# Both norm borders around a feed forward, worked in two halves of 256 tokens

## The reference, cut to what matters

```python
    h = h + rmsnorm(mixed @ w_out, g_mix_post)            # border 1, unit "wo" ahead of it
    hn = rmsnorm(h, g_ffn_pre)
    f = jnp.square(jax.nn.relu(hn @ w_ff1)) @ w_ff2       # units "f1" and "f2"
    h = h + rmsnorm(f, g_ffn_post)                        # border 2
...
    ada = silu(c) @ ada_w + ada_b                         # worked out beside the feed forward
    h = rmsnorm_2(x, norm1_g) * (1.0 + sc1) + sh1
    z = h @ w_in                                          # units "cin", "lat", "ga", "gc"
```

## Time and profile before

| | us |
|---|---|
| median of 3 runs | 1757.79 (1756.8 to 1762.38) |
| the profiled execution | 1757.74 |
| its span, first to last instruction | 1755.7 |
| mean granted TensorE clock | 0.977 |
| PE busy | 1664.1 (95%) |
| DVE busy | 1189.1 (68%) |
| ACT busy | 735.0 (42%) |
| POOL busy | 340.0 (19%) |

### The profile page before, as it was taken

How to read it: one execution, slowest core, us unless ns; L and a number is a source line. 1 busy time by engine, 2 the same in 40 slices (tenths; PEclk the granted TensorE clock), 3 DMA queues, 4 the chain that set the end, 5 groups by cost and what they waited for, 6 DMA issues and landing times. The chain is left out here.

```text
span 1755.7 us, 19580 instructions
## 1 busy us (share of the span) xinstructions
PE 1664.1 (95%) x8098; PEld 1322.3 (75%) x8098; DVE 1189.1 (68%) x1541; ACT 735.0 (42%) x955; POOL 340.0 (19%) x193
## 2 busy tenths in 40 slices
PE   5999899899999998999999988999999999999997
PEld 4878787777888886888887877878755776777775
DVE  5979768872333438953466446767965657899998
ACT  4253445444312243221222214334376237677774
POOL 1000011214100002500000004434501004445452
PEclk9999999899999998999999997999999999999999
DMA  5535223433322232445335421222210205999995
GB/s 213 194 116 167 71 64 107 149 98 121 108 96 96 96 144 100 167 165 192 143 121 192 161 104 54 73 96 96 96 44 5 73 0 212 383 386 391 385 360 189
DMA packets 59639, 264.49 MB, mean 151 GB/s; under 512 B 21648, under 2 KB 22288, under 8 KB 33056
## 3 DMA queue, kind: packets, MB, share of 16 engines
q1 hardware_dynamic: 34896, 159.10, 25.1%
q0 software_dynamic: 15184, 99.90, 14.5%
q10 hardware_dynamic: 9472, 4.26, 0.9%
HBM read 239.80 MB, written 23.44 MB: 150 GB/s over the span
## 5 line engine op out<-in xcount | busy, mean ns | idle before, releaser
L376 PE MATMUL bank<-h_high,wsplit 128*128 128x512 f32 x992 | 320.6, 401 | 10.8 <-DVE h_low L2070 4.9
L1583 DVE TENSOR_TENSOR wsplit<-ring,wsplit 128x2048 fp32r<-128x2048 f32 x75 | 174.3, 2324 | 161.3 <-ACT wsplit L968 161.2
L968 ACT ACTIVATE wsplit<-ring 128x2048 fp32r<-128x2048 f32 x98 | 187.1, 1909 | 205.2 <-PE bank L376 192.5
L376 PEld LDWEIGHTS bank<-h_high,wsplit 128*128 128x128 f32 x992 | 188.3, 190 | 57.7 <-ACT h_high L1298 5.1
L376 PE MATMUL bank<-xn_high,wsplit 128*128 128x512 f32 (+1 forms) x832 | 217.2, 348 | 12.1 <-DVE xn_low L1614 8.0
L376 PE MATMUL bank<-h_low,wsplit 128*128 128x512 f32 x496 | 197.5, 398 | 0.0
L376 PEld LDWEIGHTS bank<-xn_high,wsplit 128*128 128x128 f32 x832 | 145.6, 190 | 34.7 <-DVE xn_low L1614 8.1
L376 PE MATMUL bank<-f_high,wsplit 128*128 128x512 f32 x512 | 168.2, 401 | 0.0
L376 PE MATMUL bank<-xn_low,wsplit 128*128 128x512 f32 (+1 forms) x416 | 143.8, 346 | 0.0
L1583 POOL TENSOR_TENSOR wsplit<-ring,wsplit 128x2048 fp32r<-128x2048 f32 x23 | 106.6, 4635 | 175.6 <-ACT wsplit L968 175.5
L2617 POOL TENSOR_TENSOR x<-x,z 128x512 f32<-128x512 f32 x8 | 11.6, 1444 | 554.3 <-DVE z L2058 554.3
(11 more groups left out here) (500 smaller groups left out, 3314.9 us busy)
## 6 DMA issues: line engine op xcount, KB each, us to landing
ring<-in_W SPq DMA_DIRECT2D x122, 1024.0 KB, 4.8
weights_out<-prep SPq DMA_DIRECT2D x8, 864.0 KB, 5.2
prep<-weights_out_early POOLq DMA_DIRECT2D x8, 576.0 KB, 3.1
xslot<-zeros SPq DMA_DIRECT2D x7, 516.0 KB, 5.1
block<-xslot SPq DMA_DIRECT2D x6, 516.0 KB, 12.2
yslot<-block_out SPq DMA_DIRECT2D x6, 512.0 KB, 8.8
prep<-turns_early POOLq DMA_DIRECT2D x8, 288.0 KB, 2.4
x_in<-in_xT SPq DMA_DIRECT2D x4, 528.0 KB, 7.7
```

Source lines behind the costliest of these rows:

```text
L376: return g.matmul(o, l, r, start=first, stop=last_, skip_group_check=True)
L968: g.activation(wst[:, side(n), 0, :], ringt[:, n % RING, :], ACT.Copy).then_inc(*a.sig(("high", n)))
L1583: g.tensor_tensor(wst[:, side(n), 1, :], ringt[:, n % RING, :], hi, SUB).then_inc(*t.sig(("low", n), ("released", n)))
```

## The change

The two borders are worked in halves of 256 tokens. Ahead of border 1 the unit wo_3 is computed for z0 and then for z1, and behind it f1_0 and f1_1 go z0, z0, z1, z1 (`in_halves`). Ahead of border 2 it is f2_14 and f2_15 (f2_14 for z0 and z1, then f2_15 for both), and behind it cin_0 and cin_1 in the same pattern. The sums, roots, inverses, spreads, residuals and splits are halved alike. For z1 the sum and the spread stand on PE within the first unit behind the border, after input block 3 and block 6. The low parts of cin_1 and cin_2 move from POOL to DVE, POOL's low parts of h at border 2 move to DVE, and the positions are now loaded when the last low part of z1 is done.

```diff
-POOL_LOW = {UNIT[p] for p in [("zg", i) for i in range(4)] + [("zs", 0), ("zs", 1)] + [("cin", i) for i in (1, 2, 3)]
+POOL_LOW = {UNIT[p] for p in [("zg", i) for i in range(4)] + [("zs", 0), ("zs", 1)] + [("cin", 3)]
...
+            def sum_half(name, z, x, first=True, last=True):
+                b = fresh(name, z) if first else banks.at(name, z)
+                for m in range(2):
+                    t = mm(b[:, m:m + 1], x[:, 128 * m:128 * m + 128], ones[:, 0:1], first and m == 0, last)
+                t.then_inc(*p.sig((name, z)))
+                if last:
+                    banks.close(name, z)
+            def spread_half(name, z):
+                b = fresh(name, "scale", z)
+                p.wait_ge(*at("inverse", name, z))
+                for m in range(2):
+                    t = mm(b[:, 128 * m:128 * m + 128], rt4[:, 2 * z + m:2 * z + m + 1].to_broadcast([128, 128]), ident, True, True)
+                t.then_inc(*p.sig((name, "scale", z)))
+                banks.close(name, "scale", z)
+            def in_halves(name, xh, xl, rows, beside):
+                for z in range(2):
+                    for i in range(2):
+                        n = UNIT[name, i]
+                        wh, wl = weights(n, 8, 2048)
+                        p.wait_ge(*at("low", n))
+                        grown = [fresh(name, 2 * i + j, z)[:, 0:256] for j in range(2)]
+                        for k in range(8):
+                            p.wait_ge(*at(rows, k, z))
+                            for j in range(2):
+                                m = slice(128 * j, 128 * j + 128)
+                                t = three(grown[j], wh[:, k, m], wl[:, k, m], xh[:, k, TK[z]], xl[:, k, TK[z]], k == 0, k == 7)
+                                if k == 7:
+                                    t.then_inc(*p.sig((name, 2 * i + j, z), ("used", n)))
+                            beside(z, i, k)
+                        for j in range(2):
+                            banks.close(name, 2 * i + j, z)
...
+                        if (z, i, j) == (1, 3, 0):
+                            p.wait_ge(*at("mix_post", "square", 7, 0))
+                            sum_half("mix_post", 0, nrm[:, 2, TK[0]])
+            spread_half("mix_post", 0)
             p.end("end", "wo", "pe")
-            sum_by_token("mix_post", nrm[:, 2, :], first=7)
-            spread_scale("mix_post")
...
+            def wo_second(z, i, k):
+                if (z, i, k) == (0, 0, 3):
+                    p.wait_ge(*at("mix_post", "square", 7, 1))
+                    sum_half("mix_post", 1, nrm[:, 2, TK[1]])
+                if (z, i, k) == (0, 0, 6):
+                    spread_half("mix_post", 1)
             column = None
+            in_halves("f1", hh, hl, "h_split", wo_second)
...
+                            if (z, kg, j, k) == (1, 1, 1, 3):
+                                spread_half("ffn_post", 0)
+                        if (z, kg, j) == (1, 1, 0):
+                            p.wait_ge(*at("ffn_post", "square", 7, 0))
+                            sum_half("ffn_post", 0, nrm[:, 2, TK[0]])
...
-            spread_scale("attn_pre")
+                row_sum(k, 0)
+            spread_half("attn_pre", 0)
+            def second_half(z, i, k):
+                if (z, i, k) == (0, 0, 3):
+                    p.wait_ge(*at("ffn_post", "square", 7, 1))
+                    sum_half("ffn_post", 1, nrm[:, 2, TK[1]])
+                if (z, i, k) == (0, 0, 6):
+                    spread_half("ffn_post", 1)
+                if (z, i) == (0, 1) and k:
+                    row_sum(k - 1, 1)
+                if (z, i, k) == (0, 1, 7):
+                    row_sum(7, 1)
+                    spread_half("attn_pre", 1)
...
+            wo_rows(6, 0)
+            wo_rows(7, 0)
+            wo_rows(6, 1)
+            root_half("mix_post", 0)
             for k in range(8):
+                x_high(k, 0)
+                if k == 3:
+                    wo_rows(7, 1)
+                if k == 5:
+                    next_high("f1", 0)
+            root_half("mix_post", 1)
+            for k in range(8):
+                x_high(k, 1)
...
+            next_high("f2", 15)
+            last_square(6, 0)
+            last_square(7, 0)
+            z_root(0)
+            x_squares(0)
+            last_square(6, 1)
+            root_half("attn_pre", 0)
+            next_high("cin", 0)
             for k in range(8):
-                a.wait_ge(*at("attn_pre", "x", k))
-                square("attn_pre", k, X[:, k, :])
-            root_by_token("attn_pre")
-            a.wait_ge(*at("end", "ffn", "pe"))
+                h_high(k, 0)
+                if k == 0:
+                    last_square(7, 1)
+                if k == 4:
+                    z_root(1)
+            x_squares(1)
+            conv_rows(0, 0)
+            root_half("attn_pre", 1)
             for k in range(8):
-                a.wait_ge(*at("h2_value", k))
-                g.activation(hh2[:, k, :], mt[:, k, :], ACT.Identity, bias=ada[0][:, k:k + 1]).then_inc(*a.sig(("h2_high", k)))
-                if k % 2:
-                    g.activation(mt[:, k, :], mt[:, k, :], ACT.Identity, bias=ada[0][:, k:k + 1]).then_inc(*a.sig(("h2_shifted", k)))
+                h_high(k, 1)
+            conv_rows(1, 0)
+            next_high("cin", 1)
+            conv_rows(0, 1)
+            conv_rows(1, 1)
+            next_high("cin", 2)
...
+            def residual_half(name, after, z, gain, then=None, beside=None):
+                scale = banks.at(after, "scale", z)[:, 0:256]
+                v.wait_ge(*at(after, "scale", z))
+                for k in range(10):
+                    if k < 8:
+                        if name == "ffn_pre" and z == 0 and k % 4 == 0:
+                            v.wait_ge(res_landed[k // 4], 16)
+                        if name == "ffn_pre":
+                            v.wait_ge(*at("wo_out", k) if k < 6 else at("wo_out", k, z))
+                        v.wait_ge(*v.own())
+                        g.scalar_tensor_tensor(out=Z[:, k, TK[z]], in0=Z[:, k, TK[z]], scalar=gain[:, k:k + 1], in1=scale, op0=MUL, op1=MUL).then_inc(
+                            *v.sig((name, "z", k, z), ("free", after, "scale", z)))
+                        if k % 2 == 0:
+                            v.wait_ge(*v.own())
+                            g.tensor_tensor(X[:, k, TK[z]], X[:, k, TK[z]], Z[:, k, TK[z]], ADD).then_inc(*v.sig((name, "x", k, z)))
+                    if then and k > 1:
+                        then(k - 2)
+                    if beside:
+                        beside(k)
...
+            next_low("wo", 3)
+            for j in (6, 7):
+                sums_half("mix_post", j, 0)
+            inverse_half("mix_post", 0)
+            def between(k):
+                if k == 1:
+                    sums_half("mix_post", 6, 1)
+            residual_half("ffn_pre", "mix_post", 0, vec("g_mix_post"), lambda k: split_x(k, 0), between)
+            sums_half("mix_post", 7, 1)
+            next_low("f1", 0)
+            inverse_half("mix_post", 1)
+            residual_half("ffn_pre", "mix_post", 1, vec("g_mix_post"), lambda k: split_x(k, 1))
...
+            ada_begin(UNIT["ada", 0])
+            ada_begin(UNIT["ada", 1])
+            for z in range(2):
+                for j in range(4):
+                    f_rows(j, z)
+                    if (z, j) == (1, 1):
+                        next_low("f1", 1)
...
+            def h_rows(z, beside=None):
+                v.wait_ge(*at("attn_pre", "scale", z))
+                for k in range(9):
+                    if k < 8:
+                        h_value(k, z)
+                    if k:
+                        h_split(k - 1, z)
+                    if beside:
+                        beside(k)
...
+            next_low("f2", 15)
+            last_row(6, 0)
+            sums_half("ffn_post", 6, 0)
+            last_row(7, 0)
+            sums_half("ffn_post", 7, 0)
+            z_squares(0)
+            inverse_half("ffn_post", 0, rx)
+            residual_half("attn_pre", "ffn_post", 0, vec("g_ffn_post"))
+            ada_end(UNIT["ada", 23])
+            last_row(6, 1)
+            sums_half("ffn_post", 6, 1)
             v.wait_ge(*v.own())
             for gs, name, sc in ((g1, "norm1_g_2", ada[1]), (g2, "norm2_g_2", ada[4])):
                 g.tensor_scalar(gs, sc, 1.0, None, ADD).then_inc(*v.sig())
                 v.wait_ge(*v.own())
                 g.tensor_tensor(gs, gs, vec(name), MUL).then_inc(*v.sig())
-            v.wait_ge(*at("ffn_post"))
-            g.tensor_tensor(z4, banks.at("ffn_post")[:, 0:4], rx, MUL).then_inc(*v.sig(("free", "ffn_post")))
-            v.wait_ge(*v.own())
-            g.tensor_tensor(z4, z4, rx, MUL).then_inc(*v.sig(("z_square",)))
-            residual("attn_pre", "ffn_post", vec("g_ffn_post"), times=rx)
-            inverse_by_token("attn_pre")
-            v.wait_ge(*at("end", "ffn", "pe"))
```

(28 more changed lines are left out.)

225 lines of the change are left out of this document (149 added, 76 removed).

## The result

The changed kernel takes 1766.55 us (median of 8 runs, 1764.37 to 1768.61), the kernel before 1758.32 us beside it (8 runs, 1756.80 to 1765.64). The ratio is 1.0042 with a 95% interval of 1.003 to 1.0054, slower by 5.3 to 9.5 us.

The account below looks back on a forecast made before the run. PE, 95% busy, loses 45 us at the two borders: border 1 is bound by DVE, border 2 by a long chain through all engines. 1757.74 + 10.7 - 5.7 = 1762.7 us, range 1752 to 1770.

Parts of the forecast that it names:

- Border 1: wo_3 to f1_2 and the restart behind it: a loss of +10.7 us, bounds +6.4 to +13.
- the 0.8 taken off for roundings: Border 1: the steps gave 11.5 us, lowered to +10.7 because some roundings go one way.
- The restart: PE from f1_2's start, after its wait for the weights: lower clock costs 2.1 us, added to a loss of 9.4.
- DVE without a gap from 662 to 704: Border 1, a sign listed as what would show the forecast: DVE works without idling over that time.
- The price of a half: Instructions on 256 tokens: on PE two halves cost 0.238 for 0.233 us, on DVE 0.96 for 0.75 and 0.84 for 0.69.
- Border 2: f2_14 to cin_2: a gain of 6.2 us, with contention taken as -5.7, bounds -7.8 to +1.8.
- The mixed stretch: Border 2, PE doing cin_1's first half mixed with z1's row sums: 9.2 us, from 1067.8 to 1077.2.
- Behind it: After border 2, later positions and rope tables: cost nothing, first convolution 6 to 7 us earlier still; failing cover costs border 2's gain.
- A clock full throughout: Rival, 20%: PE never long enough without matmuls to fall to 0.50; +6.4 - 7.8 = -1.4, 1756.3 us.
- Halves that overlap as drawn: Rival, faster, 15%: DVE halves cost little over half, f1_2's split ends before PE's 694; border 1 -1, border 2 -7.8, 1749 us.
- The mixed stretch at half clock: Rival, slower, 13%: border 2's row sums hold the clock at 0.50 among cin_1's halves, 17.3 for 9.2, +8, 1770.7 us.
- the convolutions: Rival, slower, 10%: rope tables start 8 us later on DVE, first convolution no earlier than 1112, the 5.7 are lost, 1768.4 us.

Follow-up runs that it names:

- +11.1 alone: Changed kernel with border 2 whole again and the splits of cin_1 and cin_2 back on POOL: 1773.83 us, ratio 1.0081 to before.
- alone -5.2: Changed kernel with border 1 whole again as in before, border 2 still in halves: 1754.81 us, ratio 0.9977 to before.
- both early: Changed kernel with two ada units begun in DVE's wait for the second scale and f1_2's weights split after two half rows, not six: 1754.7 us, ratio 0.9981.
- three orders: both early (0.9981); that with z1's last sum and reciprocal inside z0's residual (0.9997); that with third ada unit behind f1_3's split, f1_4's between f1_2's rows (1.0001).

## Why the prediction was right

**Border 1, forecast +10.7.** Measured +11.4 and +9.5 in two profiles of the changed kernel, +11.1 alone. The parts of the sum made 11.5; the 0.8 taken off for roundings belong to no step, and the measured parts, 8.8 to f1_2 and 2.6 behind it, make 11.4. The steps, with 1.68 added to after: z0's scale was used at 661.15 (forecast 661.7), the sum of z1's squares was ready at 672.2 (673.4), z1's residual began at 678.2 (679.2) and took 10.08 (10.0), 15.4 us lay from its end to f1_2 (15.1), f1_2 started at 703.64 (704.3). PE waited 3.01 for the sum (3 to 4) and 7.44 for the weights (7). The restart was a little dearer: from f1_2's start to f2_0 69.9 us in place of 67.3, 2.6 where 2.1 stood. One sign was wrong, "DVE without a gap from 662 to 704": DVE idled 3.61 us ahead of the second half. The prediction's own working has that wait, since its sum was ready at 673.4, f1_1's split takes 2.3, and the second scale comes only at 679.2. The experiments show the mechanism: with the ada units moved ahead of the second half the wait for f1_2's weights is 4.82, with the split ahead of four of the half rows 2.92, with both none.

**The price of a half.** The Trainium skill, "VectorE: DVE Perf Modes", in the section on the TRN2 errata, advises tiles of at least 512 elements. The trace agrees here: the 16 half scalings of z take 479 to 482 ns each where a whole one takes 0.75 us, and each residual half 10.1 us or more.

**Border 2, forecast -5.7.** Measured -6.5 and -4.8, alone -5.2. Counted from f2_8 in the scale of before, which is 9.68 off here: cin_0 1056.1 (forecast 1056.5), cin_1 1067.2 (1067.8), z1's first block 1079.7 (1080.7). The mixed stretch ran at 1.00. (In the prediction 1067.8 + 9.2 is 1077.0, not 1077.2, a slip of 0.2 that is carried to the end.)

**Behind it, forecast nothing.** The first convolution started at 1115.62 in the changed kernel, 5.2 us later than in before counted from wo_0 (1112.11), which is the sum of the two borders. For the convolution the term was right. The 4.1 us behind the latents, which spoke against it at first, are there in one profile of the changed kernel and not in the other.

**The rivals.** A clock full throughout fell: in the first profile it was 0.72 and 0.50 inside f1_0, 0.71 in f1_2 and 0.78 over the row sums. Halves that overlap as drawn fell for this order; with both early, PE no longer waits for f1_2, and the kernel is 0.2% faster than before, not the 9 us of that rival, since DVE's work remains. The mixed stretch at half clock and the convolutions fell, as above.

**What is open.** The two terms were right by mechanism, and each within 1.2 us. That their sum fits so closely is luck in part, since their misses cancel (+0.7 and -0.8 in the first profile, -1.2 and +0.9 in the second); the medians differ by 3 us more than forecast all the same. The stretches give +4.9 us (+11.4 - 6.5) in the first profile of the changed kernel and +4.7 (+9.5 - 4.8) in the second, the median of the runs gives +8.2, and its interval begins at 5.3. The ratios of the other kernels also lie 0.5 us below to 3.1 us above what their stretches give. So some 3 us of the 8 are not explained. The clock in attention is a candidate and not shown: it differs by as much between executions, and of the 13 profiles of all kernels only two, one of before and one of the changed kernel, have the first scores at 3.70 us and 589.2 us behind the latents; the other eleven have 592.8 to 596.2. That the runs without a profile divide in the same way is not known.

## What to carry to other kernels

Where the engine that does the elementwise work has no idle time, halving a tile to overlap its two halves adds instructions on that engine and puts the second half ahead of the next unit's preparation. Read what stands ahead of the next unit's weights in its queue, and fill the one wait that the halves open with work that needs nothing from them. When work is moved that frees a buffer, the move is also that of the load behind it and of every load issued after that.
In a dependence chain that runs through several units, taking away one wait of PE can merely move it: three orders gave the same 149 to 150 us here. Before you explain a difference of a few us from one profile of each kernel, take a second of both.

## What the runs showed of the hardware

The granted clock over the 10 us behind the same wait of 1.83 us was 1.00 in one execution of before and 0.83 in another. The first scores, eight matmuls, took 3.70 us in two profiles, and 5.40 or 7.09 us in others, behind a wait of 2.44 to 2.46 us where it was 1.83. From the latents to the second wo2 wait three profiles of before, the same kernel, differ by up to 5 us.
The 64 row sums of one column held 0.50 for 14 us when they stood alone in before. Interleaved with halves of cin_1 they ran at 1.00 (the last window of the changed kernel's first profile).
